# FFN 2 of a transformer block: gate and up as seven products of blocks, with sums of the weights made by accumulating transfers

## The reference, cut to what matters

```python
def swiglu(h, w_gate, w_up, w_down):        # h 512 x 1024, w_gate and w_up 1024 x 2816, w_down 2816 x 1024
    return (jax.nn.silu(h @ w_gate) * (h @ w_up)) @ w_down
x = x + 0.5 * g3[:, None, :] * swiglu(h, ffn2_w_gate[l], ffn2_w_up[l], ffn2_w_down[l])
```

## Time and profile before

| | us |
|---|---|
| median of three runs | 1163.62 (1163.29 to 1167.69) |
| the profiled execution, its own time | 1163.01 |
| its span, first to last instruction | 1161.2 |
| PE busy | 1145.9 (99%) |
| DVE, ACT, POOL busy | 625.5, 451.7, 58.9 |
| moved by DMA | 151.45 MB, 130 GB/s over the span |

### The profile page before, as it was taken

One profiled execution on the slowest core, in us unless ns is written; L12 is line 12 of the kernel. 1 busy time (PEld: TensorE's weight loads), 2 busy tenths in 40 slices (PEclk: granted clock), 3 DMA queues, 4 the chain that ended last, 5 costly groups with the idle time before them and its releaser, 6 DMA issues.

```text
span 1161.2 us, 16214 instructions
## 1 busy us (share of the span) xinstructions
PE 1145.9 (99%) x5730; PEld 969.9 (84%) x5730; DVE 625.5 (54%) x1051; ACT 451.7 (39%) x709; POOL 58.9 (5%) x86
## 2 busy tenths in 40 slices
PE   8899999999999999999999999999999999999997
PEld 7788888888888998888888888899888888888887
DVE  5766666666555666776565566756433333333332
ACT  5233332332222357665555566434322222222232
POOL 3301000000000000010001010000000000000000
PEclk9999999999999999999999999999999999999999
DMA  9567566556555423343343442341333333333332
GB/s 312 162 219 243 181 218 204 174 184 211 172 172 167 110 63 102 91 125 86 90 120 96 111 117 72 91 139 37 97 98 101 90 98 101 90 93 94 99 113 74
DMA packets 221149, 151.45 MB, mean 130 GB/s; under 512 B 5078, under 2 KB 202916, under 8 KB 221108
## 3 DMA queue, kind: packets, MB, share of 16 engines
q1 hardware_dynamic: 217108, 138.76, 39.8%
q0 software_dynamic: 3280, 9.79, 3.2%
q10 hardware_dynamic: 720, 2.36, 0.6%
HBM read 148.73 MB, written 4.52 MB: 132 GB/s over the span
## 4 chain that ended last, share of the span: by engine, by line
PE 91%; DVE 2%; SPq 2%; issue 1%; DMA 1%; ACT 1%; POOL 0%; DVEq 0%; POOLq 0%; ACTq 0%
PE bank L1492 28%; PE bank L1494 28%; PE bank L1493 28%; PE bank L1827 2%; PE bank L1820 1%; SPq L446 1%; PE bank L1843 1%; PE bank L1815 1%; PE bank L1842 1%; DMA raw<-in_ffn_w_gate_dram 1%; SPq L465 1%; DMA adas<-in_ada_w_dram 1%; SPq L459 0%; DVE hL L1010 0%; DVE tmp L1005 0%
## 5 line engine op out<-in xcount | busy, mean ns | idle before, releaser
L1492 PE MATMUL bank<-hH,wH 128*128 128x512 f32 (+1 forms) x1072 | 413.2, 385 | 3.6 <-DVE hL L1010 3.1
L1494 PE MATMUL bank<-hH,wL 128*128 128x512 f32 (+1 forms) x1072 | 409.0, 382 | 0.0
L1493 PE MATMUL bank<-hL,wH 128*128 128x512 f32 (+1 forms) x1072 | 408.8, 381 | 0.0
L617 ACT ACTIVATE wH<-raw 128x1024 fp32r<-128x1024 f32 (+1 forms) x169 | 176.2, 1042 | 500.2 <-PE bank L1494 500.2
L944 DVE TENSOR_TENSOR wL<-raw,wH 128x1024 fp32r<-128x1024 f32 (+1 forms) x169 | 203.4, 1204 | 280.3 <-ACT wH L617 279.7
L1492 PEld LDWEIGHTS bank<-hH,wH 128*128 128x128 f32 x1072 | 201.6, 188 | 44.4 <-issue 5.1
L1494 PEld LDWEIGHTS bank<-hH,wL 128*128 128x128 f32 x1072 | 201.5, 188 | 39.1
L1493 PEld LDWEIGHTS bank<-hL,wH 128*128 128x128 f32 x1072 | 201.8, 188 | 37.7
L1492 PE MATMUL bank<-actH,wH 128*128 128x512 f32 (+1 forms) x332 | 126.9, 382 | 0.0
L1494 PE MATMUL bank<-actH,wL 128*128 128x512 f32 (+1 forms) x332 | 126.6, 381 | 0.0
L1493 PE MATMUL bank<-actL,wH 128*128 128x512 f32 (+1 forms) x332 | 126.6, 381 | 0.0
(11 more groups left out here) (204 smaller groups left out, 1188.6 us busy)
## 6 DMA issues: line engine op xcount, KB each, us to landing
adaw<-in_ada_w_dram SPq DMA_DIRECT2D x28, 1024.0 KB, 6.0
raw<-in_ffn_w_gate_dram SPq DMA_DIRECT2D x43, 512.0 KB, 3.8
raw<-in_ffn_w_up_dram SPq DMA_DIRECT2D x43, 512.0 KB, 3.8
raw<-in_mix_w_in_dram SPq DMA_DIRECT2D x41, 512.0 KB, 3.8
raw<-in_ffn_w_down_dram SPq DMA_DIRECT2D x32, 512.0 KB, 3.7
adas<-in_ada_w_dram SPq DMA_DIRECT2D x16, 512.0 KB, 8.2
raw<-in_ffn_w_down_dram SPq DMA_DIRECT2D x16, 384.0 KB, 3.4
raw<-in_mix_w_out_dram SPq DMA_DIRECT2D x8, 512.0 KB, 3.7
```

The costliest lines, as they stand in the source:

```text
L617: nc.scalar.activation(wH[s][:, :n * P], raw[s][:, :n * P], ACT.Copy).then_inc(hi_done, 1)
L1492: T.matmul(o, a[0], b[0], start=start, stop=False)
L1493: T.matmul(o, a[0], b[1], start=False, stop=False)
L1494: return T.matmul(o, a[1], b[0], start=False, stop=stop)
```

## The change

The matrices of gate and up are seen as 2 x 2 blocks: the 1024 input features in two halves, and the 2816 inner ones in two halves (tiles 0 to 10 and 11 to 21); the tokens are two halves of 256. A product of 2 x 2 blocks takes eight products of blocks; the change does it with seven (numbered P1 to P7), of sums of blocks of the weights by sums of blocks of h, and adds these up to the four blocks of the result.

The first two pairs of inner tiles (0 and 11, 1 and 12; `DIRECT = 2`) go as before, with eight units. For each of the other nine pairs of tiles, i and i + 11, PE makes seven products, 63 in all. One product is, for gate and for up, four tiles of weights by 256 columns, so 24 matmuls of 256 columns; gate's result takes the left half of a bank and up's the right one.

**Sums of weights.** They are made in DRAM (`wsum_d`, four sums for gate and four for up). POOL issues eight steps, each a transfer of 512 x 1408 float32 (2.88 MB) for gate and one for up, by turns a plain copy into the sum's place and an accumulating transfer that adds a block to it; a step waits until the one before has landed. They stand behind `biases_b(1)`, `biases_b(2)`, `biases_b(3)`, and each of the four `biases_a`; the last follows the seventh at once. SP waits for all of them before it loads the first product's weights.

**Sums of h.** POOL adds hH and hL up to whole blocks (`whole`, four instructions of 128 x 1024), DVE makes four sums of them (`token_sums`), ACT and DVE split these (`t_high`, `t_low`).

**Weights of a product.** SP loads them with two transfers of 256 KB (gate, up) into raw[0] or raw[1] by turns, once the low part of the product two before is made; ACT and DVE split them (`w_high`, `w_low`) into one of three slots. Both do this two products ahead of PE's.

**Sums of products.** ACT copies two of the seven banks, DVE makes seven additions, ACT two silus, DVE two multiplications, and ACT and DVE split the result as before.

**Down.** Its first two units get other places for their weights; PE waits for all 22 inner tiles ahead of the second unit. The three semaphores of POOL's table become one.

In the diff below the new code of the sums of h and of helpers is left out; a line "..." marks what is left out.

```diff
     U_OUT = U_BR[1] + DT // 2
     U_GU2 = U_OUT + DT
-    U_DN2 = U_GU2 + 2 * FT
+    HF, DIRECT = FT // 2, 2
+    U_DN2 = U_GU2 + 4 * DIRECT
     U_END = U_DN2 + 3 * DT
...
+    ORDER_P = (1, 2, 5, 6, 7, 3, 4)
+    B_P = {1: 4, 2: 7, 5: 5, 6: 6, 7: 0, 3: 1, 4: 2}
+    N_BL, N_TWOS = len(ORDER_P), HF - DIRECT
+    N_PROD = N_BL * N_TWOS
+    W_SLOTS = 3
     assert (ADA0 + ADA1) * AC + ADA2 * AC2 == N_MOD * D
...
+        def raw_slot(n):
+            return raw[(U_DN2 + n) % 2]
+        def w_slot(n):
+            q = n % W_SLOTS
+            return (wH[(U_DN2 + q) % 2], wL[(U_DN2 + q) % 2]) if q < 2 else (wH_r, wL_r)
...
+        def sp_ffn_by_blocks(sp):
+            ws = (ffn2_w_gate, ffn2_w_up)
+            for i in range(DIRECT):
+                for k in range(4):
+                    t = i + HF * (k // 2)
+                    sp_load(sp, U_GU2, 4, i, k, tiles_of(ws[k % 2], slice(t * P, (t + 1) * P)))
+            sp.wait_ge(w_summed, 16 * 16)
+            for n in range(N_PROD):
+                i, p = DIRECT + n // N_BL, ORDER_P[n % N_BL]
+                if n < 2:
+                    sp.wait_ge(lo_done, U_DN2 - 1 + n + FREE)
+                else:
+                    sp.wait_ge(w_lo, n - 1)
+                cols = slice(i * P, (i + 1) * P)
+                for m in range(2):
+                    if p in (1, 2, 4):
+                        k0, t = {1: (0, i), 2: (DT // 2, i), 4: (DT // 2, i + HF)}[p]
+                        src = tiles_of(ws[m], slice(t * P, (t + 1) * P), DT // 2, k0)
+                    else:
+                        src = wsum_d[m, {5: 0, 6: 1, 3: 2, 7: 3}[p]].rearrange("(k p) n -> p k n", p=P)[:, :, cols]
+                    half = DT // 2 * P
+                    sp.dma_start(raw_slot(n)[:, m * half:(m + 1) * half].rearrange("p (k n) -> p k n", k=DT // 2), src
+                                 ).then_inc(w_in[n % 2], 16)
+            for i in range(DT // 2):
+                for k in range(6):
+                    k0, n = PARTS[k % 3]
+                    if i == 0 and k < 2:
+                        sp.wait_ge(w_lo, N_PROD - (N_PROD - 1 - k) % 2)
+                    t = 2 * i + k // 3
+                    sp_load(sp, U_DN2, 6, i, k, tiles_of(ffn2_w_down, slice(t * P, (t + 1) * P), n, k0))
...
+            def weight_sums(step):
+                half, cols = D // 2, HF * P
+                if step:
+                    pool.wait_ge(w_summed, 32 * step)
+                for m, w in enumerate((ffn2_w_gate, ffn2_w_up)):
+                    a11, a12 = w[0, 0:half, 0:cols], w[0, half:D, 0:cols]
+                    a21, a22 = w[0, 0:half, cols:], w[0, half:D, cols:]
+                    r1, r2, r3, q1 = (wsum_d[m, q] for q in range(4))
+                    to, what = ((r1, a21), (r1, a22), (r2, r1), (r2, a11), (r3, r2), (r3, a12), (q1, a11), (q1, a21))[step]
+                    if step % 2:
+                        pool.dma_start(to, what, accum_op=ALU.add).then_inc(w_summed, 16)
+                    else:
+                        pool.dma_start(to, what).then_inc(w_summed, 16)
+            def whole(n):
+                q = (12, 11, 22, 21)[n]
+                nc.gpsimd.tensor_tensor(hB[q][:, :, :], f32(block_of(hH, q)), f32(block_of(hL, q)), ALU.add).then_inc(h_whole, 1)
...
+                    weight_sums(2 * PAIRS - 1)
+                if n == 4:
+                    pool.wait_ge(hL_done, 5 * DT)
+                    for q in range(4):
+                        whole(q)
...
+            def w_high(n):
+                act.wait_ge(w_in[n % 2], 32 * (n // 2 + 1))
+                if n < 2:
+                    act.wait_ge(unit_done, U_DN2 - 1 + n)
+                elif n >= W_SLOTS:
+                    act.wait_ge(p_done, n - W_SLOTS + 1)
+                nc.scalar.activation(w_slot(n)[0][:, :], raw_slot(n)[:, :], ACT.Copy).then_inc(w_hi, 1)
...
+            def gates(t, j):
+                act.wait_ge(c_made, 7 * t + (5, 7)[j])
+                act.wait_ge(actL_done[1], 2 * (DIRECT + t) + START)
+                nc.scalar.activation(by_halves(sg[:, j, :]), of_gate((c1, c2)[j]), ACT.Silu, scale=(1.0, -1.0)[j]).then_inc(gated, 1)
+            def two_by_blocks(t):
+                for at in range(N_BL):
+                    n = N_BL * t + at
+                    if n + 2 < N_PROD:
+                        w_high(n + 2)
+                    else:
+                        k = n + 2 - N_PROD
+                        act.wait_ge(p_done, N_PROD - N_BL + 4 + k)
+                        prep_home(U_DN2 + k, U_DN2)
+                    if t and at == 0:
+                        gates(t - 1, 1)
+                    if t and at == 1:
+                        act_high(t - 1, 0)
+                        act_high(t - 1, 1)
+                    if at == 1:
+                        act.wait_ge(p_done, n)
+                        if t:
+                            act.wait_ge(multiplied, 2 * t - 1)
+                        nc.scalar.activation(K_P1, bank[:, B_P[1], :], ACT.Copy).then_inc(kept, 1)
+                    if at == 3:
+                        act.wait_ge(p_done, n)
+                        if t:
+                            act.wait_ge(multiplied, 2 * t)
+                        nc.scalar.activation(K_P5, bank[:, B_P[5], :], ACT.Copy).then_inc(kept, 1)
+                    if at == 6:
+                        gates(t, 0)
...
+                w_high(0)
+                silu(1, 2)
+                w_high(1)
+                t_high(5, 1)
+                hi(1, 1)
+                for t in range(N_TWOS):
+                    two_by_blocks(t)
+                gates(N_TWOS - 1, 1)
...
+            def t_low(p, highs):
+                dve.wait_ge(t_hi, highs)
+                h, l = moving(p)
+                V.tensor_tensor(l, hB[{6: 22, 7: 12, 4: 21, 5: 11}[p]][:, :, :], f32(h), ALU.subtract).then_inc(t_lo, 1)
...
+            def block(t, step):
+                to, a, b, copies, made, products = (
+                    (K_U2, K_P1, bank[:, B_P[6], :], 1, 0, 4), (K_P1, K_P1, bank[:, B_P[2], :], 1, 1, 2),
+                    (K_U3, K_U2, bank[:, B_P[7], :], 1, 1, 5), (K_U2, K_U2, K_P5, 2, 3, 0),
+                    (K_U2, K_U2, bank[:, B_P[3], :], 2, 4, 6), (K_P5, K_U3, K_P5, 2, 4, 0),
+                    (K_U3, K_U3, bank[:, B_P[4], :], 2, 6, 7))[step]
+                dve.wait_ge(kept, 2 * t + copies)
+                if made:
+                    dve.wait_ge(c_made, 7 * t + made)
+                if products:
+                    dve.wait_ge(p_done, N_BL * t + products)
+                if t and step in (0, 2):
+                    dve.wait_ge(multiplied, 2 * t)
+                V.tensor_tensor(to, a, b, ALU.add).then_inc(c_made, 1)
...
+            def two_by_blocks(t):
+                for at in range(N_BL):
+                    n = N_BL * t + at
+                    if n + 2 < N_PROD:
+                        w_low(n + 2)
+                    else:
+                        prep_home(U_DN2 + n + 2 - N_PROD)
+                    if t and at == 0:
+                        block(t - 1, 6)
+                        for j in range(2):
+                            multiply(t - 1, j)
+                    if t and at == 1:
+                        for j in range(2):
+                            act_low(t - 1, j)
+                    for step in {4: (0, 1), 5: (2, 3), 6: (4, 5)}[at] if at >= 4 else ():
+                        block(t, step)
...
+                for j in range(2):
+                    lo(0, j)
+                prep(u0, 4, 1, 2)
+                token_sums(0)
+                product(1, 0)
+                prep(u0, 4, 1, 3)
+                lo(1, 0)
+                token_sums(1)
+                t_low(6, 1)
+                t_low(7, 2)
+                t_low(4, 3)
+                w_low(0)
+                w_low(1)
...
+                t_low(5, 4)
+                product(1, 1)
...
+            def gate_up_by_blocks():
+                u0 = U_GU2
+                for k in range(4):
+                    pe.wait_ge((silu_done, prod_done)[k % 2][1][k // 2], 1 + START)
+                    h_unit(4 + u0 + k, (u0 + k) % 2, bank[:, k, :]).then_inc(unit_done, 1)
+                for n in range(N_PROD):
+                    t, p = n // N_BL, ORDER_P[n % N_BL]
+                    if t and p in (1, 5):
+                        pe.wait_ge(kept, 2 * t - 1 + p // 5)
+                    elif t:
+                        pe.wait_ge(c_made, 7 * t - 7 + {6: 1, 2: 2, 7: 3, 3: 5, 4: 7}[p])
+                    elif p in (7, 4):
+                        pe.wait_ge(silu_done[1][B_P[p] // 2], DIRECT + START)
+                    elif p == 3:
+                        pe.wait_ge(prod_done[1][0], DIRECT + START)
+                    if t == 0 and p in (5, 6, 7, 4):
+                        pe.wait_ge(t_lo, {6: 1, 7: 2, 4: 3, 5: 4}[p])
+                    pe.wait_ge(w_lo, n + 1)
+                    wh, wl = w_slot(n)
+                    h, l = moving(p)
+                    for m in range(2):
```

(46 more changed lines are left out.)

135 lines of the change are left out of this document (117 added, 18 removed).

## The result

The changed kernel takes 1279.59 us (median of 4 runs, 1276.08 to 1280.18), the kernel before 1163.53 beside it: 1.0982 times as long, 95% interval 1.095 to 1.1014. The forecast was 1172.5 us, and its range ended at 1210.

A forecast was written before the change was run, and what follows sets the result against it. PE was taken as the bound, busy 1145.9 of 1161.2 us. The span of 1161.2, plus 9.5 for FFN 2 and 1.8 outside the span, gave 1172.5 us; the whole range was 1152 to 1210.

The forecast's parts named there:

- The sums in DRAM: Steps on POOL's queue: 16.9 us each, no wait for the sums under 35 us a step; counted 0.
- Rival 2: Token mixing: sums hold up raw loads, deciding from a 12.5 us step; 1209 cheap end, 1277 dear end; chance 0.25.
- PE's work: FFN 2's products: 20.16 us a pair of inner tiles instead of 21.77, a gain of 14.5 us over nine pairs.
- The round of a raw buffer: FFN 2's weight loads: 6.2 us for two products against PE's 5.76, so PE waits; 21.7 us a set.
- The page against the row: Landing of 512 KB: measured 3.8 us against the skill's 3.2, by which PE would bind; the measurement was followed.
- Rival 1: FFN 2: the halves land after 3.2 to 3.4 us, PE binds; 1154 to 1156 us; chance 0.20.
- ACT and DVE between the rounds: FFN 2: silu behind DVE's work holds buffers 0.46 us a set, rounded to 0.5; a set takes 22.2 us.
- Start and end: FFN 2: PE waits 1.5 us at the start; down's first unit at 1037.1 instead of 1029.46, its second at 1044.4.
- Sum for FFN 2: Start, nine sets and end together lengthen the span by 9.5 us.
- What would show it: Profile signs: a set at 22.2 us, landings near 3.8; token mixing over 317 us with PE waiting would mean rival 2.

The follow-up runs named there:

- e1: Kernel before plus the eight steps of sums issued by POOL at the change's places, sums unused: 1267.77 us (1 run).
- e11: Kernel before plus the sums, unused, in 64 pieces of 0.59 MB, one at a time, none beside FFN 1's last units: 1164.89 us, ratio 1.0008.
- e3: Kernel before plus the eight steps, all as plain copies, none accumulating: 1233.09 us (1 run).
- e12: The change with sums in light pieces, later order of ACT and DVE, and a third raw buffer: 1153.02 us, ratio 0.9906.
- e8: Changed kernel without the sums in DRAM, up's half of the weights loaded from POOL's queue: 1185.75 us, ratio 1.0166 to the kernel before.
- e6: Changed kernel without the sums in DRAM, with later gates in ACT's and DVE's order: 1177.79 us, ratio 1.0105 to the kernel before.
- e5: Kernel before plus one plain 5.77 MB copy from ACT's queue in 512 B rows at token mixing's start: 1179.68 us (1 run).

## Why the prediction was wrong, point by point

- **The sums in DRAM: the step that failed.** I counted 0 for them and gave the case in which they hold up token mixing a quarter. They cost 98.9 us in the changed kernel, 103.1 alone (e1), and pieces short enough cost about nothing (e11). The step asked first whether the sums are ready in time, and found slack of that; what mattered was what they do to others. Two sizes were off: 16.9 us for a step, from a stretch that moved 341 GB/s, was 21 for a plain one (two transfers of 2.88 MB, the second landed 21.3 us after its issue), which is 275 GB/s, and 32 for an accumulating one, near the top of the bounds of 16.9 and 34. The row that spoke for it was there: the raw load that landed after 5.9 us beside four small bias loads.
- **Rival 2** had the mechanism, the place and the order of size: its dear end, 1277 us, is 3 us from the result. That closeness is partly luck: it took plain steps for 16.9 us instead of 21, added FFN 2 at +9.5 instead of +17.9, and had no term for the clock, at which PE's matmuls took 21 us more in token mixing. Its point of decision, a step of 12.5 us, is borne out roughly by e1 and e3 with the measured lengths (112 and 68 against 103.1 and 68.4). The range went up only to its cheap end, which rested on 16.9 us a step; with the upper bound of the step in it, it would have reached 1277.
- **PE's work** was right to 0.01 us: 20.16 us a set forecast, 20.15 measured in e12, once nothing else binds.
- **The round of a raw buffer** was right in the ordinary case (6.2 forecast, 6.16 measured; landings 3.75 and 3.8), wrong in taking a median for a mean: 0.8 us a set more by the estimate above.
- **The page against the row.** The Trainium skill, DMA: Bandwidth & Descriptors, Anatomy of one DMA, has a fit for transfers that GpSimd issues, by which 256 KB would take 2.6 us (an estimate from it). The traces do not agree: 3.0 to 3.1 us for the first half and 3.4 for the second from SP's queue, and 3.6 from POOL's in e8. Rival 1 (PE binds with two buffers) did not come.
- **ACT and DVE between the rounds** was mis-sized: 0.46 us a set for the gate in ACT's order, 1.0 by e6. I had followed one gate; each of the two waits for DVE's additions, 20.1 / 9 = 2.2 us the first and 15.9 / 9 = 1.8 us the second in the changed kernel, and what stands behind them on ACT is a high part.
- **Start and end.** With both terms gate and up end later. PE's first matmul of down stood at 1143.72, that is 1044.9 counted from the same norm in the kernel before (less 98.9), where I had 1037.1. From there the end's norm is 2.5 us later than before; I had forecast a gap of about 2. In its place came the 2 us at the lower clock. (The terms listed for the second unit add up to 5.84, which gives 1044.1 and not 1044.4; it changes nothing.)
- **Sum for FFN 2**: +9.5 forecast, +17.9 measured. Eight sets at 1.25 more than forecast are 10.0 of the difference, less 1.6 at start and end.
- **What would show it** named the right sign for rival 2: token mixing longer than 317 us with PE waiting behind late raw loads.

## What to carry to other kernels

A background copy is not free because its own deadline is met: ask what the short-packet loads beside it get. Where queues share the engines packet by packet, as in the trace here, a 512 B stream beside 5.5 KB packets is left with a few per cent (4.0 to 9.1 in these views); cut the copy into pieces no longer than the slack of the loads, one at a time, and keep them out of stretches where loads have none. One remedy is untried: POOL's queue carried the same kind of weight loads in packets of 3.3 KB (e8, 15.73 MB in 4800), so loads from there might hold their own better beside a copy; no run shows it. And when products get shorter, count the buffers of the raw loads anew: two were enough for 5.44 us a unit, three were needed for 2.88, and the third could lie in a result that comes late.

## What the runs showed of the hardware

- An accumulating transfer from DRAM to DRAM took 1.5 times as long as a plain one: 32 us against 21 for 5.77 MB.
- Beside packets of 5.5 KB a load of 512 KB in 512 B packets landed after up to 31.4 us in the changed kernel (POOL's queue), and after 16.2 us beside a plain copy of ACT's queue; beside a copy in 512 B packets it took 7.6 us (e5, one load). Alone it takes 3.8.
- The second of two transfers of 2.88 MB in 512 B rows held its issuing engine for 10.4 us, the first for 1.4; in 5632 B rows each held it for 0.6.
- The second of a pair of 256 KB loads landed late (4.0 to 5.0 us) in 13 of 63 pairs (e6); single loads of 512 KB in the kernel before never over 3.9 in the same stretch.
- After 4.6 us without a matmul the following 4.4 us were granted 0.50, that is 1.2 GHz.
